# One decode step of a hybrid decoder: mLSTM masks on VectorE, sample outputs in four column groups, early page numbers, and a new order at both ends of GLA

## What is computed

```python
# mLSTM, one chunk (128 prompt tokens, or the 4 tokens of one sample)
d_log = jnp.where(causal, b[..., :, None] - b[..., None, :] + ic[..., None, :], -jnp.inf)
inter = b + m[..., None]
m_t = jnp.maximum(inter, jnp.max(d_log, axis=-1))
s = jnp.einsum('bhtk,bhsk->bhts', qc, kc) * jnp.exp(d_log - m_t[..., None])
w_inter = jnp.exp(inter - m_t)
num = w_inter[..., None] * jnp.einsum('bhtk,bhkv->bhtv', qc, C) + jnp.einsum('bhts,bhsv->bhtv', s, vc)
...
# GLA, one chunk
o_inter = jnp.einsum('bhtk,bhkv->bhtv', qc * jnp.exp(b), S)
a = jnp.einsum('bhtk,bhsk,bhtsk->bhts', qc, kc, jnp.exp(rel))
o = o_inter + jnp.einsum('bhts,bhsv->bhtv', a, vc)
```

## Time and profile before

| what | value |
|---|---|
| median of 3 runs | 1670.25 us (1669.08 to 1671.64) |
| profiled execution | 1670.62 us |
| its span, first to last instruction | 1669.0 us |
| mean granted clock of PE | 0.975 |
| PE busy | 1592.0 us, 95% |
| DVE busy | 877.4 us, 53% |
| ACT busy | 597.4 us, 36% |
| POOL busy | 94.3 us, 6% |
| DMA moved | 195.15 MB, mean 117 GB/s |

### The profile page before, as it was taken

The page is one execution under the profiler, slowest core; times in us unless marked ns, Lnnn a source line. Parts: engine busy times, 40 slices in busy tenths (PEclk is TensorE's granted clock), DMA queues, the critical chain, the costliest instruction groups (busy, mean ns, idle before and its releaser), DMA issues.

```text
span 1669.0 us, 31575 instructions
## 1 busy us (share of the span) xinstructions
PE 1592.0 (95%) x12446; PEld 1436.6 (86%) x12446; DVE 877.4 (53%) x1559; ACT 597.4 (36%) x963; POOL 94.3 (6%) x173
## 2 busy tenths in 40 slices
PE   7899999899989999999999999979899999999996
PEld 6799997344449999999999989978799999999995
DVE  5544455365553744444444756866746444444445
ACT  5222224346534522222332634344454322222323
POOL 0000002242320000000000000000000000000000
PEclk9999999899989999999999999989999999999998
DMA  5312116899871212212222311222322222212211
GB/s 185 116 54 79 65 67 219 311 340 337 330 253 61 98 60 96 101 71 80 101 75 76 110 55 63 91 77 112 130 77 76 76 76 101 92 61 98 93 58 56
DMA packets 50603, 195.15 MB, mean 117 GB/s; under 512 B 7405, under 2 KB 9614, under 8 KB 36690
## 3 DMA queue, kind: packets, MB, share of 16 engines
q1 hardware_dynamic: 35938, 139.49, 23.8%
q0 software_dynamic: 14576, 54.41, 8.7%
HBM read 182.19 MB, written 11.68 MB: 116 GB/s over the span
## 4 chain that ended last, share of the span: by engine, by line
PE 83%; DVE 9%; ACT 4%; issue 2%; SPq 1%; DMA 1%; POOLq 0%; POOL 0%; DVEq 0%; ACTq 0%
PE ps L309 22%; PE ps L311 22%; PE ps L310 22%; DVE wlo L298 2%; PE ps L1365 2%; PE ps L1338 1%; ACT whi L294 1%; PE ps L1531 1%; PE ps L1573 1%; PE ps L1477 1%; DVE s0b L2311 1%; SPq L1317 1%; DMA kbuf<-in_k_cache_dram 1%; PE ps L414 0%; DMA raw<-in_weights_dram 0%
## 5 line engine op out<-in xcount | busy, mean ns | idle before, releaser
L309 PE MATMUL ps<-xhi,whi 128*128 128x280 f32 x2112 | 627.2, 297 | 23.3 <-DVE wlo L518 10.9
L311 PE MATMUL ps<-xhi,wlo 128*128 128x280 f32 x2112 | 619.8, 293 | 0.0
L310 PE MATMUL ps<-xlo,whi 128*128 128x280 f32 x2112 | 618.9, 293 | 0.0
L309 PEld LDWEIGHTS ps<-xhi,whi 128*128 128x128 f32 x2112 | 402.4, 191 | 32.1 <-issue 20.8
L310 PEld LDWEIGHTS ps<-xlo,whi 128*128 128x128 f32 x2112 | 401.5, 190 | 0.5
L311 PEld LDWEIGHTS ps<-xhi,wlo 128*128 128x128 f32 x2112 | 401.5, 190 | 0.0
L298 DVE TENSOR_TENSOR wlo<-raw,whi 128x2048 fp32r<-128x2048 f32 x97 | 222.2, 2291 | 197.9 <-ACT whi L294 197.3
L294 ACT ACTIVATE whi<-raw 128x2048 fp32r<-128x2048 f32 x96 | 183.5, 1911 | 386.3 <-PE ps L311 386.3
L309 PE MATMUL ps<-dhi,whi 128*128 128x280 f32 x1024 | 300.7, 294 | 5.0 <-DVE wlo L298 4.6
L311 PE MATMUL ps<-dhi,wlo 128*128 128x280 f32 x1024 | 300.3, 293 | 0.0
L310 PE MATMUL ps<-dlo,whi 128*128 128x280 f32 x1024 | 299.4, 292 | 0.0
(11 more groups left out here) (408 smaller groups left out, 1457.9 us busy)
## 6 DMA issues: line engine op xcount, KB each, us to landing
raw<-in_weights_dram SPq DMA_DIRECT2D x98, 1024.0 KB, 4.8
kbuf<-in_k_cache_dram SPq DMA_DIRECT2D x128, 256.0 KB, 5.2
vbuf<-in_v_cache_dram POOLq DMA_DIRECT2D x128, 256.0 KB, 8.4
s0b<-in_gla_in_dram POOLq DMA_DIRECT2D x4, 1024.0 KB, 5.1
out_dram<-s0b POOLq DMA_DIRECT2D x4, 1024.0 KB, 4.5
hT<-in_x_dram SPq DMA_DIRECT2D x2, 1120.0 KB, 9.1
out_dram<-pj POOLq DMA_DIRECT2D x2, 1120.0 KB, 8.6
hT<-in_x_dram POOLq DMA_DIRECT2D x2, 1120.0 KB, 13.3
```

What stands on the lines that cost most here:

```text
L309: pe.matmul(out, whi[:, par, t, :], hi, start=first, stop=False)
L310: pe.matmul(out, whi[:, par, t, :], lo, start=False, stop=False)
L311: return pe.matmul(out, wlo[:, par, t, :], hi, start=False, stop=last)
```

## The change

Five edits are made at once.

- mLSTM masks: PE only broadcasts the decays. DVE adds the mask into `dec` (chunks, then samples), copies the decay factors `wdh` in place of ACT, and signals `m_msk`; ACT takes the exponentials in place from there.
- Sample outputs: sample s goes to column group s mod 4 (32 rows each) of bank 6, two samples to a group. DVE copies the four groups to `gq`; at n = 4 PE multiplies `gq` by `four` (four identities of 32 on top of one another, made in `cols_dve`), which adds the groups; DVE's gated addition moves from n = 3 to n = 4 and signals `m_it4`, which PE awaits at n = 5.
- `load_keys` reads the page numbers of sample 1 ahead of the wait for the slab's split.
- GLA, start: pieces 0 and 1 come ahead of the first turn, piece 2 behind it. DVE does piece 0's eviction, `last_k`, piece 1's eviction, and only then the low part of the pair's last slab, which the odd projection did before (`split1`). Head 2 has one piece in place of two.
- GLA, end: while head 3's last steps run, PE does six of the eight `k` of the first out1 output (`out1_ahead_pe`), in bank 6 (banks 0 and 6 swap roles in out1). The mix is split in three parts (heads 0 and 1, head 2, head 3); each part's first token half is split early, the second halves come at the end. `mlp_pe` of layer 1 awaits output 14's eviction.

Unseen in the diff's core: semaphores of the gate and the normalization are renumbered to free names, and `out_act` and `out_pe` use `out_bank`.

```diff
@@ build
+        gq = at("gq", o - 2560, [P, P + 1])
+        four = at("four", o, [P, N_SAMP]); o += 128
...
+        def out_bank(name, n):
+            return {0: 6, 6: 0}.get(n % 8, n % 8) if name == "out1" else n % 8
...
@@ mlp_pe
+            if L:
+                pe.wait_ge(S["o_ev"], 16 * POST[out] + 15)
@@ odd_dve
+                pair_dve(..., split1=i < LAST - 1)
...
@@ cols_dve
+            own.link(dve.tensor_tensor(four[:, :], ident[:, 0:32], ident[:, 32:64], ALU.add))
+            own.link(dve.tensor_tensor(four[:, :], four[:, :], ident[:, 64:96], ALU.add))
+            own.link(dve.tensor_tensor(four[:, :], four[:, :], ident[:, 96:128], ALU.add))
@@ mlstm_pe, n == 0
-                pe.matmul(ps[:, 7, :], sel, rows[:, R_RM, 0:SEQ], start=True, stop=False)
-                for c in range(4):
-                    pe.matmul(ps[:, 7, c * P:(c + 1) * P], ident, cst[:, C_NEG:C_NEG + P], start=False, stop=c == 3)
-                pe.matmul(ps[0:T4, 6, 0:T4], sel[:, 0:T4], rows[:, R_RM, SEQ:N_TOK], start=True, stop=False)
-                pe.matmul(ps[0:T4, 6, 0:T4], ident[0:T4, 0:T4], cst[0:T4, C_NEG4:C_NEG4 + T4], start=False, stop=True)
+                pe.matmul(ps[:, 7, :], sel, rows[:, R_RM, 0:SEQ], start=True, stop=True)
+                pe.matmul(ps[0:T4, 6, 0:T4], sel[:, 0:T4], rows[:, R_RM, SEQ:N_TOK], start=True, stop=True)
@@ mlstm_pe, n == 3
-                    mm = pe.matmul(third(6, 2)[0:N_SAMP], qm[:, N_SAMP * s:N_SAMP * (s + 1)], c0[h % 2][:, s, :],
-                                   start=s == 0, stop=s == DEC_B - 1)
+                    g = 32 * (s % 4)
+                    mm = pe.matmul(third(6, 2)[g:g + 32], qm[:, N_SAMP * s:N_SAMP * (s + 1)], c0[h % 2][:, s, :],
+                                   start=s < 4, stop=s >= 4)
@@ mlstm_pe, n == 4, ahead of the wait on m_C
+                pe.wait_ge(S["m_hx"], h + 1)
+                pe.matmul(third(6, 2)[0:N_SAMP], four[:, :], gq[:, :], start=True, stop=True)
@@ mlstm_dve, n == 0, ahead of the wait on m_tr
+                dve.wait_ge(S["m_bc"], h + 1)
+                dve.tensor_tensor(dec[:, 0:SEQ]..., ps[:, 7, :]..., cst[:, C_NEG:C_NEG + P]..., ALU.add)
+                dve.tensor_tensor(dec[0:T4, SEQ:N_TOK], ps[0:T4, 6, 0:T4], cst[0:T4, C_NEG4:C_NEG4 + T4], ALU.add)
+                dve.tensor_copy(wdh[:, :], ps[:, 6, 64:76]).then_inc(S["m_msk"], 1)
@@ load_keys
+            numbers = page_numbers(sp_, 0, 1)
             sp_.wait_ge(S["lo"], SLAB0["out0"] + 3)
             load_first(sp_, 1, SLAB0["out0"] + 1)
-            load_k(sp_, 0, 1, page_numbers(sp_, 0, 1), range(4))
+            load_k(sp_, 0, 1, numbers, range(4))
@@ gla_pe
             piece_pe(pe, 0, range(KB))
+            piece_pe(pe, 1, range(KB))
             gla_turn_pe(pe, 0)
             gla_turn4_pe(pe, 0)
-            piece_pe(pe, 1, range(KB))
+            piece_pe(pe, 2, range(KB))
...
-                if h < 3:
-                    piece_pe(pe, 2 + 2 * h, range(KB))
+                if h < 2:
+                    piece_pe(pe, 3 + 2 * h, range(KB))
...
-                    piece_pe(pe, 3 + 2 * h, range(KB))
+                    piece_pe(pe, min(4 + 2 * h, 7), range(KB))
+                else:
+                    out1_ahead_pe(pe)
                 gla_back_pe(pe, h)
...
+        def out1_ahead_pe(pe):
+            pe.wait_ge(S["lo"], SLAB0["out1"] + 3)
+            pe.wait_ge(S["ev"], EV["odd"] + 8 * LAST + 8)
+            for k in range(6):
+                mix_wait_pe(pe, 0, k)
+                product(pe, ps[:, 6, 0:HALF], 0, k, xhi[:, k, COLS[0]], xlo[:, k, COLS[0]], k == 0, False)
+        def out1_first_pe(pe):
+            for k in range(6):
+                product(pe, ps[:, 1, 0:HALF], 0, KB + k, ...)
+            for k in range(6, KB):
+                mix_wait_pe(pe, 0, k)
+                ...
+            for h, par in ((0, 1), (1, 0), (1, 1)):
+                if h == 0:
+                    pe.wait_ge(S["lo"], SLAB0["out1"] + 4)
...
@@ gla_end_act
+            gla_mix_hi(act, 2, 0)
+            for part in range(3):
+                gla_mix_hi(act, part, 1)
             act.wait_ge(S["done"], DONE["out1"])
             split_hi(act, SLAB0["out1"] // 2, 1)
@@ gla_dve
             level_pick(dve, 7)
+            piece_dve(dve, 0)
             last_k(dve)
+            piece_dve(dve, 1)
+            split_lo(dve, LAST + SLAB0["odd"] // 2, 1)
...
+                if h == 3:
+                    gla_mix_lo(dve, 1, 0)
                 gla_carry_dve(dve, h)
...
+                if h == 2:
+                    gla_mix_lo(dve, 0, 0)
+            gla_mix_lo(dve, 2, 0)
+            for part in range(3):
+                gla_mix_lo(dve, part, 1)
             split_lo(dve, SLAB0["out1"] // 2, 1)
```

More of the change, by code:

```diff
@@ L1139, in mlstm_dve @@
                 dve.wait_ge(S["m_in"], h + 1)
-                own.link(dve.tensor_copy(hx[0:T4, 4, :], third(6, 1)[0:T4]))
-                dve.scalar_tensor_tensor(hx[0:N_SAMP, 4, :], third(6, 2)[0:N_SAMP], gate(4, W_)[0:N_SAMP],
-                                         hx[0:N_SAMP, 4, :], ALU.mult, ALU.add)
+                dve.tensor_copy(gq[:, :], third(6, 2))
+                dve.tensor_copy(hx[0:T4, 4, :], third(6, 1)[0:T4])
                 dve.tensor_copy(hx[:, 3, :], third(6, 0))
@@ L1147, in mlstm_dve @@
                 dve.wait_ge(S["m_hx"], h + 1)
+                dve.scalar_tensor_tensor(hx[0:N_SAMP, 4, :], third(6, 2)[0:N_SAMP], gate(4, W_)[0:N_SAMP],
+                                         hx[0:N_SAMP, 4, :], ALU.mult, ALU.add).then_inc(S["m_it4"], 1)
                 for c in range(4):
@@ L2230, in gla_act @@
                     gla_values_act(act, h + 1)
+                    if h == 2:
+                        act.wait_ge(S["done"], DONE["out1"])
+                        gla_mix_hi(act, 0, 0)
                     gla_gate_act(act, h + 1)
@@ L2235, in gla_act @@
                 if h == 2:
[L2236 to L2248, removed]
@@ L2250, in gla_end_act, with gla_mix_hi @@
-        def gla_end_act(act):
[L2252 to L2257, removed]
+                    gla_mix_hi(act, 1, 0)
+        MIX = [slice(0, 4), slice(4, 6), slice(6, 8)]
+        def gla_mix_hi(act, part, half):
+            ks = MIX[part]
+            act.wait_ge(S["h_mix"], part + 3)
+            act.activation(xhi[:, ks, COLS[half]], pj[:, VC:VC + 8, :][:, ks, COLS[half]], ACT.Copy).then_inc(S["mx_hi"], 1)
@@ new lines, in gla_mix_lo, with mix_wait_pe @@
+        def gla_mix_lo(dve, part, half):
+            ks = MIX[part]
+            dve.wait_ge(S["mx_hi"], 2 * POST["out1"] + 3 * half + part + 1)
+            dve.tensor_tensor(xlo[:, ks, COLS[half]], pj[:, VC:VC + 8, :][:, ks, COLS[half]],
+                              xhi[:, ks, COLS[half]].bitcast(f32), ALU.subtract).then_inc(S["mx_lo"], 1)
+        def mix_wait_pe(pe, h, k):
+            if k in (0, 4, 6):
+                pe.wait_ge(S["mx_lo"], 2 * POST["out1"] + 3 * h + max(0, k // 2 - 1) + 1)
@@ new lines, in out1_ahead_pe @@
+        def out1_ahead_pe(pe):
[6 more added lines that the diff above has]
+            for k in range(6):
+                product(pe, ps[:, 1, 0:HALF], 0, KB + k, xhi[:, k, COLS[0]], xlo[:, k, COLS[0]], k == 0, False)
+            for k in range(6, KB):
+                mix_wait_pe(pe, 0, k)
+                for f, b in enumerate((6, 1)):
+                    mm = product(pe, ps[:, b, 0:HALF], 0, f * KB + k, xhi[:, k, COLS[0]], xlo[:, k, COLS[0]], False, k == KB - 1)
+                    if k == KB - 1:
+                        mm.then_inc(S["done"], 1)
+            for h, par in ((0, 1), (1, 0), (1, 1)):
+                if h == 0:
+                    pe.wait_ge(S["lo"], SLAB0["out1"] + 4)
+                for k in range(KB):
+                    if h and par == 0:
+                        mix_wait_pe(pe, 1, k)
+                    for f in range(2):
+                        mm = product(pe, ps[:, out_bank("out1", 4 * h + 2 * par + f), 0:HALF], par, f * KB + k,
+                                     xhi[:, k, COLS[h]], xlo[:, k, COLS[h]], k == 0, k == KB - 1)
+                        if k == KB - 1:
+                            mm.then_inc(S["done"], 1)
```

85 lines of the change are left out of this document (41 added, 44 removed).

## The result

The changed kernel takes 1645.16 us (median of 4 runs, 1641.94 to 1647.23) against 1669.66 (4 runs, 1665.48 to 1671.64): a ratio of 0.9856, 95% interval 0.9829 to 0.9883, 24.5 us less. The profiled execution's span fell from 1669.0 to 1645.6 us.

The account below looks back on a forecast made before the run. TensorE (PE), busy nearly throughout, was taken to bound the kernel. Gains of 12.0 (heads), 4.1 (page numbers) and 8.4 (GLA), 24.5 us together, from the profiled 1670.6 gave 1646.1 us; range 1638 to 1656.

Parts of the forecast that it names:

- the prediction's own sign: Wrong if DVE's masks, the K pages or a slab show up as PE's releaser with more than 2 us a time.
- Mask products off PE: mLSTM heads: removing mask products and two further passes from PE saves 1.31 us a head, 5.2 in all.
- Column groups: mLSTM heads: sample products fall from 1.89 to 0.55 us, 1.34 a head; the adding product costs 0.25 a head.
- rival B: mLSTM heads: column groups do not overlap, 1.34 us a head lost again, 1651.5 us; chance 0.08.
- Clock, −3.0 in heads 1 and 2: mLSTM heads: with a shorter opening block, heads 1 and 2 run at head 3's pace, 1.5 us less each.
- rival A: mLSTM heads: clock falls in all heads, 3.0 us not gained and 1.5 lost, 1650.6 us; chance 0.18.
- Page numbers, 4.1: Attention start: page DMAs issued up to 8.8 us sooner, limited by shared DMA engines; 4.1 us gained (0 to 7.6).
- rival E: Further clock falls vanish as phases shift, three at 1.7 us, giving 1641 us; chance 0.06.
- GLA's start, 6.3 and 3.3: GLA start: head 0's chunks come 6.3 us sooner; head 2's missing piece saves 3.3 more, head 3 begins 9.5 early.
- GLA's end: GLA end: third output begins 10.1 us sooner despite a new 4.2 wait; clock costs 1.7, leaving 8.4 gained (5 to 11).
- Rival D: GLA: the chain of DVE or ACT holds the gain to half, 4.2 us lost, 1650.3 us; chance 0.08.
- G: GLA and attention: another engine's wait replaces the old one, nothing gained there; with A and B about 1668 us; chance 0.02.

Follow-up runs that it names:

- later masks: Changed kernel with VectorE's mask addition repeated into scratch, two further times in heads 0 and 1, five in heads 2 and 3; no total time given.
- V behind K: Changed kernel with POOL issuing sample 0's V pages only after sample 1's K pages have landed: 1645.79 us, ratio 0.9857 to the kernel before.

## Why the prediction came out

The forecast was 1646.1 against 1645.16 measured, with 24.5 us of gain forecast and measured. The step that failed is PE's wait for K pages, and by the prediction's own sign, since these pages show up as PE's releaser with 4.3 us at a time, where more than 2 was to mean wrong. By its steps:

- **Mask products off PE**, 1.31 a head: right, 1.33 by the run with masks alone (39.45 to 38.12). The cover of 1.6 us was 1.65, and the run with later masks showed that it is cover: two additions free, five not.
- **Column groups**, 0.55: right, 0.58. They overlap; rival B is out. The adding product was under-sized by 0.09. Together 0.77 a head where 1.09 was forecast; some 0.2 of that stands in no single row.
- **Clock, −3.0 in heads 1 and 2**: this step was wrong in its ground. The two falls of the first profile were counted as the kernel's. They are an execution's: five of fifteen heads over five profiles, in two executions. That masks off PE end them fits the record (none in eight profiles) and isn't shown by it; their coming in every head, rival A, is out. Of the 10.7 us that the even projection gave in this pair of profiles, 3.1 are the two falls that the first profile happened to have. Of the Trainium skill's rule on transposes ("TensorE: Matmul & The Clock Gate", Part 4) no run shows the effect that rival A drew from it: the opening now is broadcasts and transposes without mask products, and the granted clock is 1.00 in the row of 125.00 to 128.40. Five falls in five profiles are one an execution, so that list and falls account for 5.2 + 1.5 = 6.7 of the 11.7 that the masks alone gained by the times; the interval begins at 9.0. At least 2 us of it have no row, and their cause stays open.
- **Page numbers, 4.1**: that shared DMA limits the gain was right, and the size was 2.4 to 2.5 in the profiles, but the mechanism failed. SP's late issue is not why PE waits: the issue came 9 us sooner and PE's waits for K pages went from 7.6 to 8.4. The rate behind it failed too, "at that rate 9.45 MB take 24.6 us": the changed kernel's 30 us again ran at 315 GB/s, with 388 only in the middle. V behind K showed that K pages, V pages and the next samples' K pages stand in one another's way. The 2.4 us came from PE's clock: 2.7 less busy time and no less idle time up to the first V product. The step had put the clock at nothing; only rival E had further falls vanish. Why an earlier issue shortens the time at 0.50 isn't shown.
- **GLA's start, 6.3 and 3.3**: right. Head 0's chunks begin at 1102.92, 9.6 us behind piece 0's end at about 1093.3 (forecast 10.0, before 16.4); measured against the odd projection's end the gains are 6.8 and, in head 2, 3.5. The chain shows it:

```profile
1102.92 1.90 PE ps L2118 x8
...
1168.20 0.45 PE ps L2172 x2
```

- **GLA's end**: the last transposes came 25.7 us before the old ones, 1.5 more than head 3's lead at its chunks; forecast was 0.9 more. The wait (3.7) and its clock (a stretch at 0.50) came as worked out. The total of 10.6 against 8.4 is the sum of these small surpluses and of 1.0 that came ahead of GLA, in the odd projection's last pair. Moving the last slab's low part out of that pair isn't the cause: with GLA's edits alone the pair gave nothing (a lead of 4.0 ahead of it and 3.9 behind). What differs is an idle time of PE ahead of L1883, for which the profile shows no releaser: 2.1 us before, 2.2 with GLA's edits alone, 1.0 in the changed kernel. No step had it. Rival D is out.

That the gain came out to 0.1 us is luck. Two errors cancel, 3.0 too much in the heads and attention together and 2.2 too little in GLA, and three of the terms were met by something else than forecast: falls that the first profile happened to have, a clock in place of a wait, an idle time ahead of GLA. The rivals also have a slip: G by itself, nothing gained at GLA or attention, is 1658.6 by the prediction's own terms, which lies outside "between 1641 and 1651.5" and is not "same".

## What to carry to other kernels

Before a DMA is issued earlier, count all bytes that PE needs in that stretch: here an issue 9 us earlier left PE's idle time as it was, and putting one tile's pages first moved the wait to another tile's. Where PE's list is the pace, moving work to an engine with cover is worth its rows, and the cover can be measured by filling it. When an order removes a wait, look at what the next wait is made of: here two lists had the urgent split behind work that PE needed 6 us later, and turning them round gave another 3.6 us by the profile, beside the 10.6. When a forecast's sum is met, compare it term by term: here it was met twice, each time with terms that were not.

## What the hardware showed beyond that

The same head code took 41.0 us in heads 1 to 3 of one execution (granted clock 0.96) and 39.45 in heads 1 and 2 of another (1.00). One profile is not enough to price a fall of the clock. The wait of 3.7 us at out1 was followed by 3.4 us at 0.50 in all seven profiles that have it, in one of them by 6.8; in the two with the wait cut to 1.5 no such stretch came behind it. Of two waits of 2.0 in the heads, one was followed by such a stretch and one was not.
